# Summing expert rows: fourteen pairs of experts read back early, the last two added by matrix products

## The chip, the core and the metric

The kernel runs on one core of one Trainium2 chip. Time is the device time of an execution in microseconds (us); what counts is the median of several runs. TensorE is called PE, VectorE DVE, ScalarE ACT, GpSimd POOL and SyncE SP, as the profile does.

## The reference, cut to what matters

One transformer block on 512 tokens of width 1024 in f32: modulation from a conditioning vector, an RWKV-7 mixer and a sparse attention mixer, their gated merge, and a mixture of 32 experts, of which each token takes 2.

```python
def hier_moe(u, w_rg, b_rg, w_re, b_re, w_gate, w_up, w_down):
    ...
    top_v, top_i = lax.top_k(in_grp, EXPERT_TOPK)        # 2 of the 8 experts of the best group
    comb = grp_w * jax.nn.softmax(top_v, axis=-1)        # the two weights of a token
    ...
    def expert_block(args):
        xblk, e = args
        hid = jax.nn.silu(xblk @ w_gate[e]) * (xblk @ w_up[e])   # 1024 -> 512
        return hid @ w_down[e]                                   # 512 -> 1024
    ...
    y = jax.ops.segment_sum(yb * buf_w[:, None], buf_tok, num_segments=N + 1)[:N]
...
h = h + gt2 * hier_moe(u2, ...)
return rmsnorm(h, norm_final_g)
```

## The kernel before

The program is a row of blocks (stages) in which each engine has its own list of instructions, ordered by semaphores that are written out by hand. The last stage holds the merge of the mixers, the router, the experts and the final norm; most of the change is in it.

**Tiles of tokens.** The 512 tokens are NT = 4 tiles of 128. `h` keeps the residual, one row of 1024 per token.

**Router.** DVE computes for each token and each of its two choices an entry: a block and a place in that block. Blocks 0 to 15 are pairs of experts (64 places for each of the two), blocks 16 to 30 are spare ones for experts with more than 64 tokens (overflow). From one-hot tables (`at_place`, `oh_blk`) and bf16 products on PE come the tables `slots` (which token lies in place p of block b) and `y_at` (in which of the 1024 rows of `y_dram` its result belongs: choice j, token t). Overflow is counted into `over` (`r_ov`); `further` (L1806) holds a loop over the 15 spare blocks for every engine, skipped by a branch when the count is 0, as it is here. The tables of the router lie in `uT`, which is also the ninth slot of the ring of weights.

**Experts.** For each of 16 pairs `b`: POOL gathers the 128 token rows (`gather`, L1895), PE transposes them (`tokens`, L2354), multiplies by the gate and up weights (`product`, L2368), two experts at a time in the two column halves of the array, ACT applies silu, DVE multiplies (`gated`, L2171), PE transposes the hidden rows (L2378), ACT copies them (L1983), PE multiplies by the down weights (`down`, L2388) in two column halves of 512, DVE multiplies each half by the modulation row into `yo` (`finish`, L2180), and POOL stores the rows of the pair into `y_dram` by an indirect transfer (`store`, L1902).

**Order of weights.** SP issues 96 loads of 2 MB, in order, into a ring of nine slots (`load_expert`, L1786). Each waits until its slot is given back (`unit_free`); the first round waits for other things: the ninth slot for `r_ent` and `r_ov`, since the router's tables lie there. Everything on SP stands in one list, so a load that waits holds back all that follow.

**End.** When all 16 stores have landed, SP passes the overflow branch and reads `y_dram` back in eight loads `ya[2i + j]` of 512 KB (tile i, choice j), into `uT` and `mg`. For each tile DVE adds both with the token's weights into `h` (`summed`, L2216 and L2218), ACT squares and takes a root (L2006, L2008), DVE norms into `ya[2i]` (`normed`, L2224) and SP writes it out (L1876).

The first stage streams the modulation and input weights; POOL loads small parameters there and then waits until about 195 us. `vrep` is a 128x512 buffer of zeros, set by POOL near 37 us and written by DVE much later, in the compressed attention part (L679).

## Time and profile before

| | |
|---|---|
| median of 3 runs | 1309.2 us (1309.09 to 1310.15) |
| profiled execution, time | 1306.26 us |
| profiled execution, span | 1304.4 us |
| mean granted clock of PE | 0.918 |
| PE busy | 1125.7 us (86%) |
| DVE / ACT / POOL busy | 388.4 / 219.2 / 162.6 us |
| mean transfer rate | 231 GB/s |

The span is the time from the first to the last instruction of the profiled execution. Busy time of PE is that of instructions that overlap in a pipeline, so a high share of it doesn't yet say that PE is the limit. An engine's idle time is put down to what it waited for last. A matrix product in f32 shows as two records.

### The profile page before, as it was taken

The numbers are of one execution on the slowest core, as the hardware profiler recorded it, in microseconds if no ns is written. First come the engines' busy times: TensorE is split into PE (matmuls) and PEld (weight loads), VectorE is DVE, ScalarE is ACT, GpSimd is POOL, SyncE is SP. The second block draws the span as 40 slices with busy tenths as digits, with TensorE's granted clock in tenths as the row PEclk, the third lists the DMA queues.
The fourth block names the chain that finished last, engine by engine and source line by source line (L and its number), as shares of the span: only waits on it lengthen the run. The fifth ranks groups of instructions, "written<-read, shape, count | busy, mean of one in ns | idle before, by whom it ended". The sixth has DMA issues, their size and how long they took to land. (4 is left out here: it accounts for less than half of the span.)

```text
span 1304.4 us, 16842 instructions
## 1 busy us (share of the span) xinstructions
PE 1125.7 (86%) x7213; PEld 583.3 (45%) x7213; DVE 388.4 (30%) x644; ACT 219.2 (17%) x443; POOL 162.6 (12%) x211
## 2 busy tenths in 40 slices
PE   6999999999998897989899993988988878887771
PEld 5543344644555555979645451333323333333330
DVE  3244427233005444345522335111111101111105
ACT  4011213221003552424200120000000000000002
POOL 2100001050102443223100000010000000000000
PEclk7899999799996997989899995989989998888995
DMA  9512534325605000000082536999999999999975
GB/s 363 201 65 96 200 114 169 129 85 184 183 26 136 1 1 26 4 2 4 19 311 96 219 124 263 400 428 427 427 427 427 429 426 427 428 427 427 427 297 204
DMA packets 56757, 295.17 MB, mean 226 GB/s; under 512 B 8755, under 2 KB 15253, under 8 KB 43113
## 3 DMA queue, kind: packets, MB, share of 16 engines
q1 hardware_dynamic: 48362, 278.02, 53.3%
q0 software_dynamic: 6016, 11.87, 2.5%
q10 hardware_dynamic: 2304, 4.20, 0.8%
q8 instruction: 58, 0.95, 0.3%
q14 instruction: 17, 0.14, 0.0%
HBM read 284.61 MB, written 16.79 MB: 231 GB/s over the span
## 5 line engine op out<-in xcount | busy, mean ns | idle before, releaser
L2368 PE MATMUL ps<-ring,zrT 128*64 128x512 f32 x704 | 169.4, 638 | 33.3 <-issue 30.4
L894 PE MATMUL ps<-ring,uT 128*128 128x512 f32 x384 | 168.6, 596 | 0.6 <-PE ps L825 0.6
L2388 PE MATMUL ps<-ring,hdT 128*64 128x512 f32 x352 | 122.4, 632 | 6.0 <-issue 4.0
L2368 PEld LDWEIGHTS ps<-ring,zrT 128*64 128x64 f32 x704 | 58.1, 146 | 135.6 <-issue 135.1
L885 PE MATMUL ps<-uT,ring 128*128 128x512 f32 x256 | 115.1, 608 | 2.0 <-DVE uT L619 1.4
L894 PEld LDWEIGHTS ps<-ring,uT 128*128 128x128 f32 x384 | 72.1, 191 | 91.5 <-issue 91.5
L2171 DVE TENSOR_TENSOR zrT<-zrT,ps 128x512 f32<-128x512 f32 x16 | 11.0, 687 | 289.0 <-PE ps L2368 289.0
L2368 PE MATMUL ps<-mg,zrT 128*64 128x512 f32 x160 | 73.2, 612 | 7.4 <-issue 7.4
L885 PEld LDWEIGHTS ps<-uT,ring 128*128 128x128 f32 x256 | 49.0, 194 | 67.4 <-issue 66.4
L1977 ACT ACTIVATE zrT<-ps 128x512 f32<-128x512 f32 x16 | 9.6, 597 | 412.6 <-PE ps L2368 412.6
L1902 POOL DMA_INDIRECT y_dram<-zrT,y_at x16 | 16.3, 1017 | 437.1 <-DVE zrT L2180 437.1
L2388 PEld LDWEIGHTS ps<-ring,hdT 128*64 128x64 f32 x352 | 37.8, 146 | 56.1 <-issue 55.7
L2312 PE MATMUL ps<-ring,uT 128*128 128x512 f32 x128 | 55.8, 593 | 0.0
L969 POOL TENSOR_SCALAR prob<-prob,gate,rsum 128x512 f32<-128x512 f32 (+3 forms) x64 | 40.2, 639 | 117.1 <-DVE rsum L1023 116.2
L2180 DVE TENSOR_TENSOR zrT<-ps,mod 128x512 f32<-128x512 f32 x32 | 22.1, 692 | 106.0 <-PE ps L2388 106.0
L2368 PE MATMUL ps<-mod,zrT 128*64 128x512 f32 x80 | 38.0, 631 | 7.1 <-issue 7.1
L587 DVE SCALAR_TENSOR_TENSOR acc<-ring,csil,acc 128x512 f32<-128x512 f32 x56 | 42.2, 753 | 2.0
L2354 PE MATMUL ps<-cst,zrT 128*128 128x128 f32 x128 | 22.0, 325 | 23.7 <-DMA zrT<-u_dram,slots 23.7
L2388 PE MATMUL ps<-uT,hdT 128*64 128x512 f32 x80 | 37.7, 627 | 4.2 <-issue 4.2
L1046 ACT ACTIVATE prob<-ps,mx 128x512 f32<-128x512 f32 (+3 forms) x64 | 33.2, 523 | 44.8 <-DVE mx L1019 44.5
L2388 PE MATMUL ps<-mod,hdT 128*64 128x512 f32 x80 | 39.2, 647 | 0.0
L1019 DVE TENSOR_REDUCE mx<-ps 128x2 f32<-128x1024 f32 (+3 forms) x32 | 26.4, 824 | 36.9 <-PE ps L1100 36.7
(383 smaller groups left out, 1478.0 us busy)
## 6 DMA issues: line engine op xcount, KB each, us to landing
ring<-in_moe_w_gate_dram SPq DMA_DIRECT2D x22, 2048.0 KB, 30.0
ring<-in_moe_w_up_dram SPq DMA_DIRECT2D x22, 2048.0 KB, 33.6
ring<-in_moe_w_down_dram SPq DMA_DIRECT2D x22, 2048.0 KB, 32.7
ring<-in_w_in_dram SPq DMA_DIRECT2D x8, 2048.0 KB, 13.9
ring<-in_w_ada_dram SPq DMA_DIRECT2D x8, 2048.0 KB, 9.2
mod<-in_moe_w_up_dram SPq DMA_DIRECT2D x5, 2048.0 KB
mg<-in_moe_w_up_dram SPq DMA_DIRECT2D x5, 2048.0 KB, 30.8
uT<-in_moe_w_down_dram SPq DMA_DIRECT2D x5, 2048.0 KB, 36.0
```

Source lines behind the costliest of these rows:

```text
L587: link(dve.scalar_tensor_tensor(a, w[:, k, :], csil[:, k:k + 1], a, ALU.mult, ALU.add))
L885: ins = pe.matmul(ps[:, n % 4, :], slot(name, KD, w)[:, k, c0:c0 + P], uT[:, k, :], start=(k == 0), stop=(k == KD - 1))
L894: ins = pe.matmul(ps[:, n % 4, :], uT[:, k, P * i:P * i + P], w, start=(k == 0), stop=(k == KD - 1))
L969: ins = pool.tensor_scalar(p_, p_, gate[:, i, h3:h3 + 1], rsum[:, t % 4, g:g + 1], ALU.mult, ALU.mult)
L1019: dve.tensor_reduce(mx[:, t % 4, :], ps[:, 2 * (t % 2):2 * (t % 2) + 2, 0:rows_of(t)], AX, ALU.max, negate=True).then_inc(a_mx, 1)
L1046: ins = act.activation(prob[t % 4][:, g, 0:n], ps[:, 2 * (t % 2) + g, 0:n], ACT.Exp, bias=mx[:, t % 4, g:g + 1], accum_out=rsum[:, t % 4, ...
L1902: pool.indirect_dma_start(y_dram, bass.IndirectOffsetOnAxis(ap=y_at[:, b:b + 1], axis=0), yo[:, b % 2, :], None, bounds_check=2 * T - 1, o ...
L2180: dve.tensor_tensor(yo[:, b % 2, 512 * c:512 * c + 512], ps[:, 2 + c, :], mod[:, 5, 512 * c:512 * c + 512], ALU.mult).then_inc(e_y, 1)
L2312: ins = pe.matmul(ps[:, 4 + n % 3, :], mgT[:, k, P * i:P * i + P], slot(f"wo{k // 4}", 4, D)[:, k % 4, 512 * j:512 * j + 512], start=(k == ...
L2354: ins = pe.transpose(ps[:, 4 + k // 4, P * (k % 4):P * (k % 4) + P], src[:, k, :], ident)
L2368: ins = pe.matmul(ps[HALF * r:HALF * r + HALF, "gu".index(kind), :], xgT[:, b % 2, k, HALF * r:HALF * r + HALF], w[r][:, k, :], start=(k = ...
L2388: ins = pe.matmul(ps[HALF * r:HALF * r + HALF, 2 + c, :], hdT[:, j, HALF * r:HALF * r + HALF], w[r][:, j, 512 * c:512 * c + 512], start=(j ...
```

## The change

1. The eight loads of `ya` are issued by SP right after the last weight load, as soon as the stores of pairs 0 to 13 have landed and the slots `uT` and `mg` are given back. Pairs 14 and 15 are no longer stored.
2. `y_dram` is filled with zeros at the start, from `vrep`, by one POOL transfer of 4 MB, since the rows of the last two pairs are read without being stored.
3. The router also makes `w_at` (the weight of each place of each block), by splitting the weights into three bf16 parts and 24 products, and `tok_at`. The load into the ninth slot waits for these products (`r_wt`) in place of `r_ent`.
4. `places` builds for pairs 14 and 15 a matrix place x token that holds the weight where the place has that token; PE multiplies it with `yo` of these pairs. The sums of tile 3 go by PE too, with the two weights on diagonals.
5. DVE does `summed(0)` between the two halves of the last `finish`, `summed(1)` and `summed(2)` behind it, and then `whole(i)`, which adds PE's products from two banks.
6. The last down weights are loaded by column halves, and the last `down` waits for each half apart.
7. The overflow loop (not entered here) adds by the same kind of products.

```diff
+                pool.wait_ge(c_v0, 2)
+                pool.dma_start(y_dram.rearrange("(p b) (a d) -> p (b a) d", p=P, a=2),
+                               vrep[:, :].unsqueeze(1).to_broadcast([P, 4 * T // P, 512])).then_inc(c_fill, 16)
...
                 elif turns == 0 and s_ == 8:
-                    eng.wait_ge(r_ent, 1)
+                    eng.wait_ge(r_wt, 1)
                     eng.wait_ge(r_ov, 1)
...
-                load_expert(sp, "d", NPAIR - 1)
+                for c in range(2):
+                    for half in range(2):
+                        s_, turns = place_of("d", NPAIR - 1, half)
+                        if c == 0:
+                            sp.wait_ge(unit_free[s_], turns + fills[s_])
+                        sp.dma_start(expert_slot(s_, 4)[:, :, 512 * c:512 * c + 512],
+                                     dn[2 * NPAIR - 2 + half][:, :, 512 * c:512 * c + 512])\
+                            .then_inc((unit_in[s_], d_rest[half])[c], 16)
+                for q_ in range(2):
+                    sp.wait_ge(y_st[q_], 16 * (NPAIR // 2 - 1))
+                    s_, turns = place_of("g", NPAIR - 1, q_)
+                    sp.wait_ge(unit_free[s_], turns + 1 + fills[s_])
+                for i in range(NT):
+                    for j in range(2):
+                        sp.dma_start(ya[2 * i + j], y_rows[i, j]).then_inc(f_in[2 * i + j], 16)
...
                     if b + 2 < NPAIR:
                         gather(b + 2)
-                    store(b)
+                    if b < NPAIR - 2:
+                        store(b)
...
+                link(TT(w_blk[:, :, :], oh_blk[:, :, :], wts[:, :, :].rearrange("p j i -> p (j i)").unsqueeze(2)
+                        .to_broadcast([P, 2 * NT, NBLK]), ALU.mult))
+                for m in range(2):
+                    link(dve.tensor_copy(w_part[:, m, :, :], w_blk[:, :, :]))
+                    link(TT(w_blk[:, :, :], w_blk[:, :, :], w_part[:, m, :, :], ALU.subtract))
+                dve.tensor_copy(w_part[:, 2, :, :], w_blk[:, :, :]).then_inc(r_wp, 1)
...
+                def places(b):
+
+                    e_link(dve.scalar_tensor_tensor(toks[:, :], C("tile_down")[:, 0:NT], float(P),
+                                                    tok_at[:, b:b + 1].to_broadcast([P, NT]), ALU.mult, ALU.add))
+                    e_link(TT(matrix(b), C("iota").unsqueeze(1).to_broadcast([P, NT, P]),
+                              toks[:, :].unsqueeze(2).to_broadcast([P, NT, P]), ALU.is_equal))
+                    e_link(TS(matrix(b), matrix(b), w_at[:, b:b + 1], None, ALU.mult))
+                    dve.sem_inc(e_mat, 1)
...
+                finish(NPAIR - 1, 0)
+                summed(0)
+                finish(NPAIR - 1, 1)
+                for i in range(1, NT - 1):
+                    summed(i)
...
+                def whole(i):
+                    dve.wait_ge(f_c, i + 1)
+                    dve.tensor_tensor(h[:, i, :], h[:, i, :], two_banks(i), ALU.add).then_inc(f_h, 1)
...
+                        if b == NPAIR - 1 and c:
+                            for half in range(2):
+                                pe.wait_ge(d_rest[half], 16)
...
                 tokens(0)
+                pe.wait_ge(r_wp, 1)
+                for m in range(3):
+                    for n in range(2 * NT):
+                        ins = pe.matmul(ps[:, 3, 2 * NBLK:3 * NBLK], at_place[:, n, :], w_part[:, m, n, :],
+                                        start=(m + n == 0), stop=(m == 2 and n == 2 * NT - 1))
+                ins.then_inc(r_wt, 1)
...
+                further(pe, first, body, last)
+                pe.wait_ge(e_y, 2 * NPAIR)
+                pe.wait_ge(e_mat, 2)
+                for i in range(NT):
+                    if i == NT - 1:
+                        pe.wait_ge(e_diag, 2)
+                        for j in range(2):
+                            pe.wait_ge(f_in[2 * i + j], 16)
+                    for c in range(2):
+                        cols = slice(512 * c, 512 * c + 512)
+                        terms = [(diag[:, j, :], ya[2 * i + j][:, cols]) for j in range(2)] if i == NT - 1 else []
+                        terms += [(matrix(b)[:, i, :], yo[:, b % 2, cols]) for b in (NPAIR - 2, NPAIR - 1)]
+                        for m, (one, rows) in enumerate(terms):
+                            ins = pe.matmul(ps[:, bank_of[i] + c, :], one, rows, start=(m == 0), stop=(m == len(terms) - 1))
+                    ins.then_inc(f_c, 1)
```

## Rows read from the trace of the kernel before

**Rows 1.** The page, GB/s moved in each of 40 slices of 32.6 us.

```profile
GB/s 363 201 65 96 200 114 169 129 85 184 183 26 136 1 1 26 4 2 4 19 311 96 219 124 263 400 428 427 427 427 427 429 426 427 428 427 427 427 297 204
```

**Rows 2.** Who SP waited for, whole span: us in total, times, longest.

```profile
SPq L1808 <- DMA y_dram<-zrT,y_at: 44.2, 1, 44.2
```

**Rows 3.** Windows: length; PE, PEld, DVE, ACT, POOL busy; PE clock; transfer share, GB/s.

```profile
1252.00:1253.00 1.00, 1.00 (x7) 0.38 (x5) 0.00 (x0) 0.00 (x0) 0.00 (x0) 1.00 1.03 426
...
1261.00:1262.00 1.00, 1.00 (x8) 0.47 (x6) 0.00 (x0) 0.00 (x0) 0.00 (x0) 1.00 0.46 197
...
1286.00:1287.00 1.00, 0.00 (x0) 0.00 (x0) 0.96 (x2) 0.00 (x0) 0.00 (x0) 0.50 1.00 397
```

**Rows 4.** Timeline, last products: start, duration, engine, line, operation, [idle before, releaser].

```profile
1258.42 7.09 PE L2388 MATMUL ps<-ring,hdT 128*64 128x512 f32 x32 [2.68 <-issue]
...
1268.20 7.09 PE L2388 MATMUL ps<-ring,hdT 128*64 128x512 f32 x32 [2.01 <-DMA ring<-in_moe_w_down_dram]
...
1266.23 0.60 ACT L1983 ACTIVATE hdT<-ps 128x512 f32<-128x512 f32 x1 [19.57 <-PE ps L2378]
...
1275.54 0.69 DVE L2180 TENSOR_TENSOR zrT<-ps,mod 128x512 f32<-128x512 f32 x1 [2.95 <-PE ps L2388]
```

**Rows 5.** Timeline of POOL, SP and DVE behind them.

```profile
1237.29 1.02 POOL L1902 DMA_INDIRECT y_dram<-zrT,y_at  x1 [28.25 <-DVE zrT L2180]
...
1281.27 0.33 SPq L1870 DMA_DIRECT2D uT<-y_dram  x1
...
1297.08 1.28 DVE L2218 SCALAR_TENSOR_TENSOR h<-mg,wts,h 128x1024 f32<-128x1024 f32 x1
...
1300.11 1.28 DVE L2224 SCALAR_TENSOR_TENSOR uT<-h,frt,mod 128x1024 f32<-128x1024 f32 x1
```

**Rows 6.** From issue to landing: the 16 stores and 8 row loads; the first row load.

```profile
DMA to landing us min/median/max: 3.2/10.3/11.3
...
uT<-y_dram SPq DMA_DIRECT2D x1, 512.0 KB, 3.6
```

**Rows 7.** Timeline of PE, first stage: products with 128 columns of weights.

```profile
70.54 20.84 PE L885 MATMUL ps<-uT,ring 128*128 128x512 f32 x48 [0.30 <-PE ps L885]
```

**Rows 8.** The overflow branch's first instruction: duration in ns, start.

```profile
L1809 PEldq TENSOR_LOAD <-over x1: 489/489/489, 1270.8 to 1270.8; - x1
...
L1809 DVEq TENSOR_LOAD <-over x1: 547/547/547, 1275.6 to 1275.6; - x1
```

**Rows 9.** Windows of the first stage, columns as in rows 3.

```profile
40.00:42.00 2.00, 2.00 (x3) 0.71 (x3) 2.00 (x6) 0.00 (x0) 0.00 (x0) 0.50 1.02 306
...
48.00:50.00 2.00, 2.00 (x6) 0.85 (x5) 0.00 (x0) 0.32 (x1) 0.00 (x0) 1.00 1.06 389
```

**Rows 10.** Timeline at the router's end: DVE, PE, SP.

```profile
796.08 0.41 DVE L2132 TENSOR_TENSOR uT<-cst,uT 128x248 f32<-128x248 f32 x1
...
801.30 0.42 DVE L2159 CAST over<-uT 1x16 int32<-1x16 f32 x1
...
797.66 0.40 PE L2345 MATMUL ps<-uT 128*128 128x31 bf16 x8
803.78 1.97 PE L2354 MATMUL ps<-cst,zrT 128*128 128x128 f32 x8 [5.72 <-DMA zrT<-u_dram,slots]
807.16 15.40 PE L2368 MATMUL ps<-ring,zrT 128*64 128x512 f32 x64 [1.41 <-DVE zrT L2163]
...
801.82 0.33 SPq L1786 DMA_DIRECT2D uT<-in_moe_w_down_dram  x1
815.78 0.33 SPq L1786 DMA_DIRECT2D ring<-in_moe_w_down_dram  x1
```

**Rows 11.** Windows there, columns as in rows 3.

```profile
780.00:785.00 5.00, 1.63 (x8) 1.49 (x7) 2.96 (x13) 0.21 (x1) 0.00 (x0) 0.50 0.98 414
...
808.00:810.00 2.00, 2.00 (x8) 0.79 (x6) 0.00 (x0) 0.00 (x0) 0.00 (x0) 0.50 0.75 297
...
812.00:814.00 2.00, 2.00 (x12) 0.78 (x10) 0.00 (x0) 0.00 (x0) 0.00 (x0) 1.00 0.01 4
```

More of the change, by code:

```diff
@@ L1753, in build @@
         order = (1, 2, 0, 5, 3, 4, 6, 7, 8)
-        x_clear, r_ya, r_ent = sem("x_clear"), sem("r_ya"), sem("r_ent")
+        x_clear, r_ya, r_ent, r_wp, r_wt = (sem(n) for n in ("x_clear", "r_ya", "r_ent", "r_wp", "r_wt"))
+        e_mat, e_diag, e_wat, e_dve, f_c = (sem(n) for n in ("e_mat", "e_diag", "e_wat", "e_dve", "f_c"))
+        d_rest = [sem(f"d_rest{n}") for n in range(2)]
+        v_tok, v_wt, v_m1, v_m2, v_m, v_cm, v_c = (sem(f"v_{n}") for n in "tok wt m1 m2 m cm c".split())
         y_rows = y_dram.rearrange("(j i p) d -> i j p d", j=2, p=P)
@@ L1860, in body @@
                     sp.sem_inc(v_seen, 1)
-                def last():
-                    sp.wait_ge(v_st, 16 * OVER)
-                for q_ in range(2):
-                    sp.wait_ge(y_st[q_], 16 * (NPAIR // 2))
-                further(sp, first, body, last)
-                for i in range(NT):
-                    for j in range(2):
-                        sp.dma_start(ya[2 * i + j], y_rows[i, j]).then_inc(f_in[2 * i + j], 16)
+                further(sp, first, body)
                 sp.wait_ge(m_wr, 80)
@@ L2141, in _ @@
                 dve.tensor_tensor(slots[:, :], hi[:, :], ps[:, 2, 0:NBLK], ALU.add).then_inc(r_sl, 1)
+                link(dve.scalar_tensor_tensor(tok_at[:, :], hi[:, :], -float(T), ps[:, 2, 0:NBLK], ALU.add, ALU.add))
                 dve.wait_ge(r_ent, 1)
@@ L2171, in gated, with finish @@
                     dve.tensor_tensor(hd, act_g, ps[:, 1, :], ALU.mult).then_inc(e_hd, 1)
-                def finish(b):
-                    for c in range(2):
+                def finish(b, *one):
+                    for c in one or range(2):
                         dve.wait_ge(e_d, 2 * b + c + 1)
@@ L2190, in _, with summed @@
                     finish(b - 1)
-                finish(NPAIR - 1)
+                    if b == NPAIR - 2:
+                        dve.wait_ge(e_wat, 1)
+                        places(NPAIR - 2)
+                        places(NPAIR - 1)
+                        for j in range(2):
+                            dve.tensor_scalar(diag[:, j, :], C("ident"), wts[:, j, NT - 1:NT], None, ALU.mult)\
+                                .then_inc(e_diag, 1)
+                f_link = Chain(dve, f_dve)
+                def summed(i):
+                    for j in range(2):
+                        dve.wait_ge(f_in[2 * i + j], 16)
+                        f_link(dve.scalar_tensor_tensor(h[:, i, :], ya[2 * i + j], wts[:, j, i:i + 1], h[:, i, :], ALU.mult,
+                                                        ALU.add))
+                finish(NPAIR - 1, 0)
[3 more added lines that the diff above has]
+                    summed(i)
                 def first():
-                    for q_ in range(2):
-                        dve.wait_ge(y_st[q_], 16 * (NPAIR // 2))
+                    pass
                 def body(v):
@@ L2224, in normed @@
                     dve.scalar_tensor_tensor(ya[2 * i], h[:, i, :], frt[:, i:i + 1], gf, ALU.mult, ALU.mult)\
                         .then_inc(f_o, 1)
-                summed(0)
+                whole(0)
                 for i in range(1, NT):
-                    summed(i)
+                    whole(i)
                     normed(i - 1)
```

83 lines of the change are left out of this document (57 added, 26 removed).

## The prediction

> **What bounds the kernel now.** I read the transfer line of the page first. From 820 us on it stands near 427 GB/s in every slice [rows 1]: the sixteen pairs of experts are bound by the stream of their weights, and PE, though busy on the page, waits for it. What comes before sets when that stream starts, what comes after is added to its end. So I read two places: the head of the last stage, and everything behind the last weights. The matrix "who waited for whom" of SP's queue gives the second: after its last weight load SP sits 44.2 us in the wait for the stored rows [rows 2].
>
> The windows of the tail show that the last weights don't end at once: 426 GB/s at 1252 and 197 at 1261 [rows 3]. Some of the 16 transfer engines are done long before the slowest, and have nothing to do, since the rows are only asked for at 1281. The timeline then gives the chain [rows 4, 5]: the down product of the last pair starts at 1268.20, released by its weights, and ends near 1275.3; DVE scales its second half at 1275.54; POOL stores it; SP reads all rows back from 1281.27; DVE adds two rows to each of four tiles (1.28 us each), the last add starts at 1297.08 and ends at 1298.37; the last normed tile ends at 1301.39, and the span ends at 1304.4, 3.05 later.
>
> **The change at the end, part by part.** *Last down weights by halves.* The 4.19 MB of the last pair's down weights are the last in the queue. At 427 GB/s they take 9.8 us, so they arrive from 1258.4 to 1268.2. In runs of 2 KB the only rows I have are those of the first stage, 389 GB/s at 48 to 50 [rows 9]: 10.8 us, end 1269.2. The other bound is the 306 GB/s at 40 to 42, where small transfers were mixed in: 13.7 us, end 1272.1. I take the first, since nothing small is queued at the end. The first column half is there by 1265.3 even by the slow bound, before the transposed hidden rows, which ACT delivers at 1266.83 [rows 4]. So the first half of the product starts at 1266.9 instead of 1268.2, the second follows 3.55 us later, at 1270.45, if its weights are there (they are, by 1.3 us; by the slow bound they are 1.7 late, which would cost 1.7). DVE began its second half 7.34 us after the product's start [rows 4]: 1266.9 + 7.34 = 1274.2, against 1275.54. **Gain 1.3.**
>
> *Rows of fourteen pairs fetched early.* The store of pair 13 is issued at 1237.29, and stores land within 11.3 us [rows 5, 6]: SP can issue the eight row loads from 1248.6 at the latest, some 4 us in all. They stand in the queue behind the weights, so the fast engines take them in the tail that now is empty, and the slowest at 1269.2. A load of 0.52 MB at 397 GB/s [rows 3] takes 1.3 us: the first two land at 1270.5 and 1271.8, the eighth at 1279.7.
>
> *A wait is added on DVE.* It runs: first half of the last pair (2.95 + 0.69 before the second [rows 4], so 1270.6 to 1271.3), then the sums of tile 0, which wait for these two loads, then the second half of the last pair. The two sums take 2 x 1.31 = 2.6: 1273.9, and the second half is due at 1274.2. No loss, with 0.3 to spare in DVE's time and 0.8 in the landing of the second load (1271.8 against 1272.6). Behind that wait stand the second half and so PE's final products. The second half ends at 1274.9. Tiles 1 and 2 are summed to 1280.1; the branch on the overflow count then costs DVE 1.0 (its load of 0.55 and three register steps, which before lay beside the last scaling [rows 8]): DVE is free at 1281.2.
>
> *Final place-token products.* They take the place of two stores, and PE had nothing to do there. A 128x512 product with 128 columns of weights in f32 shows as two records; 48 records took 20.84 us [rows 7], 0.433 each. Tiles 0 to 2 have 4 products, tile 3 has 8, since both sums of tile 3 go by products too: 20 products, 40 records, 17.5 us with the last one's end. PE starts when both halves are scaled, at 1274.95; its own branch runs ahead of the matmuls in flight. Tiles are ready at 1278.6, 1282.0, 1285.5 and **1292.5**. DVE adds tile 0 from 1281.2 and the next two with their norms by 1289.6, so the fourth waits for PE: the path is PE's. An add of 128x1024 from the products' bank is priced between 1.28 (the SBUF form [rows 5]) and 2 x 0.69 [rows 4], I take 1.28: 1293.8. From the last sum's end to the end of the last normed tile were 3.02 us (1298.37 to 1301.39), and 3.05 to the span's end; nothing of that changes: 1293.8 + 3.02 + 3.05 = **1299.9**, against 1304.4. **Sum: -4.5 us.** So the early fetch removes the store, its landing and the read, about 10 us, and PE's products give back more than half of it.
>
> **The change elsewhere.** *Fill of the row buffer (4.2 MB written by POOL after its set-up loads, in the second slice).* A slice of 32.6 us can carry 13.9 MB at 427 GB/s; the second and third carry 6.6 and 2.1 [rows 1]. So it fits, and PE's input products, which run on from 70.54 with no wait for a transfer [rows 7], keep their cover. Its end is waited for at the reuse of its source only in the attention part. Cost 0.
>
> *Weights by entry in the router.* DVE gets one op before the count (0.2) and six of 0.41 (248 elements a partition [rows 10]) after the count's last op at 801.30: ready at 804.4. PE gets 24 bf16 products of 31 columns behind the first transposes, which end at 805.75; 8 such took 0.40, so 1.0 to 1.2: done at 806.9. PE then waited for DVE's copy until 807.16 anyway [rows 10]. Cost 0; bounds 0 and +0.5 if a weight load isn't hidden. The eighth slot's load, though, waits for them: it moves from 801.82 to 807.0. The next load is only issued at 815.78, when the first gate product gives its slot back, and from 810 the transfers stand still (4 GB/s at 812 to 814 [rows 11]): 2.1 MB need 5 us and are there by 814. Cost 0, and the price if that cover were gone is up to 5.2 us, since all later weights queue behind.
> *Masks, diagonals* on DVE before the last gated product: some 3 us between the scaling of pair 13 and the gating of pair 15, with two products of PE as long as the 7.09 us of [rows 4] in between. Cost 0.
>
> The profiled execution took 1306.26 us for a span of 1304.4; the median of the runs is 1309.2, 2.9 above it. I apply the difference to the median: 1309.2 - 4.5 = **1304.7**.
>
> **The Trainium skill.** At the head, the granted clock is 0.50 until 810 and full after it [rows 11], while PE was busy from 803.78 to 805.75 and again from 807.16 [rows 10]; the 24 new products fill the hole. The Trainium skill, "TensorE: Matmul & The Clock Gate", Part 1, says that the clock is throttled by default and that activity releases it; by that rule the hole filled may bring the full clock before the gate product, which is the rival early clock below. [...]
> For the tail, the same notes (the Trainium skill, "DMA: Bandwidth & Descriptors", Latency and other measured facts) say that two of the sixteen engines are usually slower; the falling rate of [rows 3] agrees that some are, and the sum above already takes the slowest.
>
> **Rivals.** *Early clock:* 2.9 us of the first gate product at full instead of half speed (807.16 to 810.1) bring the release at 815.78, and with it the whole stream, 1.5 forward: 1303.2. For: the hole is filled. [...] 0.2.
> *Rows late:* the sums of tile 0 hold the last scaling back. If the first row load lands 3.6 us after the last weights, as the first one did on empty queues [rows 6], the second lands at 1274.1, the last half is scaled 1.2 later: 1305.9; at worst some 2 more. For: the slowest engine decides. Against: queued loads landed at the pace of the stream. 0.15.
> *A clock drop in the final products:* PE pauses 0.7 us before and 1.0 us after the last down product; before, pauses of 2.0 and 2.7 [rows 4] left the clock full. One short stretch at half speed costs 1.7 to 2.5: 1306.4 to 1307.2. 0.1.
> *Slower, by the clock:* if the clock stays low, the products take twice 17.5 us. It decides from a low stretch of 9 us on (half of it is lost, against 4.5 gained); all of it gives 1322. For it: PE's clock drops once it is idle. Against it: no long pause is left. 0.07.
> *The slot's load delays the stream:* decides if the entry products end after 811 (their rows late, POOL's gather late). Up to 1309.9. 0.05.
> *The change doesn't do what it says:* the early row loads aren't early, because SP gets to them late, or the product of tile 3 isn't the last thing DVE waits for. Then PE's 17.5 us stand behind the loads: about 1308. 0.03.
> The forecast has the remaining 0.4.
>
> **The numbers.** Likeliest 1304.7. The range takes the early clock and 0.7 of scatter below (1302.5), and above the late rows and a clock drop together with the router's 0.5: 1304.7 + 1.2 + 2.5 + 0.5 = 1308.9 (the slow bound of the halves, 1.7, lies within). A measurement of this kernel tells some 0.2% from no change, 2.6 us: faster means below 1306.6. Forecast and early clock are there, most of the late rows, and a part of the drop: 0.72. Within 0.2%: 0.19. Slower: the low clock and the larger part of the unknown: 0.09.
>
> **What would show it.** (1) The last scaling on DVE near 1274.2, behind two sums of tile 0 with at most a few tenths of waiting for rows. (2) The final products: 40 records in about 17.5 us at full clock, starting within 0.2 us of the last scaling, and DVE's fourth add released by PE. (3) No loads of weights later at the head: the issue now at 815.78 unmoved (or 1.5 earlier: early clock). (4) The transfer rate high up to 1270 and beyond instead of falling from 1254. Wrong would be: PE waiting for tile 3's rows, the clock at 0.5 in the products, or the first gate product starting later than 807.2.

## The result

| kernel | median | lowest to highest | ratio, 95% interval |
|---|---|---|---|
| before, beside it | 1309.68 us (4 runs) | 1309.09 to 1310.17 | |
| after | 1302.05 us (4 runs) | 1301.26 to 1303.23 | 0.9943 [0.9925, 0.996] |

The change makes the kernel 7.6 us faster. The forecast was 1304.7 us, 4.5 faster, with a range down to 1302.5: the direction was right, the gain was larger than the whole range allows. The profiled execution of after took 1302.55 us for a span of 1300.7, at a mean granted clock of 0.935.

### The profile page after: what moved, and what is told of

The parts are those of the page before. It is cut to its first block and busy times, and to the rows that moved or that the text cites. A ratio compares the mean times of both kernels' runs of the same rounds, so it can differ in the third digit from the quotient of the medians.

```text
span 1300.7 us, 16995 instructions
## 1 busy us (share of the span) xinstructions
PE 1137.6 (87%) x7277; PEld 589.9 (45%) x7277; DVE 396.5 (30%) x662; ACT 218.7 (17%) x443; POOL 161.8 (12%) x210
## 5 line engine op out<-in xcount | busy, mean ns | idle before, releaser
L2448 PE MATMUL ps<-ring,zrT 128*64 128x512 f32 x704 | 163.2, 618 | 28.5 <-issue 26.3
```

Of the source, the lines that this page charges most:

```text
L2448: ins = pe.matmul(ps[HALF * r:HALF * r + HALF, "gu".index(kind), :], xgT[:, b % 2, k, HALF * r:HALF * r + HALF], w[r][:, k, :], start=(k = ...
```

## The profile after

The transfer line of the page, one number for 32.5 us, answers [rows 1].

```profile
GB/s 365 330 65 97 197 108 180 129 74 189 190 24 139 1 1 26 4 3 4 5 326 57 250 92 279 363 429 431 428 430 429 428 430 428 429 431 429 430 391 147
```

Two things are seen at once. The second slice carries 330 instead of 201 GB/s, which is the fill. And the slices of the weight stream, which the change doesn't touch, stand at 428 to 431, where before they stood at 426 to 429. I had read this line only for "the stream is the bound"; half of the surprise is in its last digit.

The head, timelines of SP and of PE [rows 10]:

```profile
807.69 0.33 SPq L1799 DMA_DIRECT2D uT<-in_moe_w_down_dram  x1
818.29 0.33 SPq L1799 DMA_DIRECT2D ring<-in_moe_w_down_dram  x1
```

```profile
806.81 0.85 PE L2479 MATMUL ps<-uT 128*128 128x31 bf16 x24
808.43 6.79 PE L2448 MATMUL ps<-ring,zrT 128*64 128x512 f32 x18 [0.76 <-DVE zrT L2199]
```

The 24 new products take 0.85 us inside the hole before the gate product; the ninth slot's load goes out at 807.69 (807.0 was forecast). The clock in the gate product (windows, columns as in rows 3):

```profile
812.00:814.00 2.00, 2.00 (x8) 0.66 (x6) 0.00 (x0) 0.00 (x0) 0.00 (x0) 0.52 0.99 424
814.00:816.00 2.00, 2.00 (x12) 0.72 (x10) 0.00 (x0) 0.00 (x0) 0.00 (x0) 1.00 0.55 221
```

It stays at half speed until nearly 814. In the profile of before it was full in 812 to 814 already [rows 11]; a second profile of the same kernel (before_again, below) has it as late as after has, with 0.60 in that stretch, and starts its gate product and the next load of weights as late:

```profile
808.62 3.68 PE L2368 MATMUL ps<-ring,zrT 128*64 128x512 f32 x8 [1.41 <-DVE zrT L2163]
818.24 0.33 SPq L1786 DMA_DIRECT2D ring<-in_moe_w_down_dram  x1
```

The last products and the final ones, PE's timeline [rows 4]:

```profile
1249.52 8.78 PE L2448 MATMUL ps<-ring,zrT 128*64 128x512 f32 x32 [2.64 <-issue]
1259.27 7.09 PE L2471 MATMUL ps<-ring,hdT 128*64 128x512 f32 x32 [0.96 <-issue]
1266.28 0.75 PE L2458 MATMUL ps<-cst,zrT 128*128 128x128 f32 x4
1267.95 7.09 PE L2471 MATMUL ps<-ring,hdT 128*64 128x512 f32 x32 [0.92 <-ACT hdT L2011]
```

DVE's timeline over the same stretch and to the end [rows 4, 5]:

```profile
1271.64 0.69 DVE L2216 TENSOR_TENSOR zrT<-ps,mod 128x512 f32<-128x512 f32 x1 [4.35 <-PE ps L2471]
1272.25 1.28 DVE L2253 SCALAR_TENSOR_TENSOR h<-uT,wts,h 128x1024 f32<-128x1024 f32 x1
1273.56 1.29 DVE L2253 SCALAR_TENSOR_TENSOR h<-mg,wts,h 128x1024 f32<-128x1024 f32 x1
1275.27 0.69 DVE L2216 TENSOR_TENSOR zrT<-ps,mod 128x512 f32<-128x512 f32 x1 [0.42 <-PE ps L2471]
...
1282.73 2.35 DVE L2299 TENSOR_TENSOR h<-h,ps 128x1024 f32<-128x1024 f32 x2 [1.61 <-issue]
...
1293.49 1.22 DVE L2299 TENSOR_TENSOR h<-h,ps 128x1024 f32<-128x1024 f32 x1 [2.64 <-PE ps L2547]
...
1296.45 1.28 DVE L2304 SCALAR_TENSOR_TENSOR uT<-h,frt,mod 128x1024 f32<-128x1024 f32 x1
```

And the chain that ended last, same stretch (start, length, what):

```profile
1275.27 0.70 DVE zrT L2216
1275.97 0.04 issue
1276.02 17.45 PE ps L2547 x40
1293.47 0.02 issue
1293.49 1.23 DVE h L2299
```

The final products stand in it as one piece of 17.45 us. SP's queue, behind the last gate and up loads:

```profile
1226.91 31.55 SPq L1879 DMA_DIRECT2D ring<-in_moe_w_down_dram  x4
1258.64 2.27 SPq L1888 DMA_DIRECT2D uT<-y_dram  x1
...
1265.36 0.60 SPq L1888 DMA_DIRECT2D mg<-y_dram  x1
```

The row loads go out from 1258.64, not from 1248.6, since the last down weights, by halves, hold the queue. The line of 31.55 us joins four issues; behind the first lies a wait for a free slot, and the third alone takes 18.24 us (the four by themselves, shortest, median and longest in ns):

```profile
L1879 SPq DMA_DIRECT2D ring<-in_moe_w_down_dram x4: 557/1773/18237, 1226.9 to 1255.6; - x4
```

The rows land 10.9 to 14.0 us after their issue, the first two loads at 1270.8 and 1271.9 us and the eighth at 1279.4, where 1270.5, 1271.8 and 1279.7 were forecast. The transfer rate of the tail against [rows 3]:

```profile
1261.00:1262.00 1.00, 1.00 (x8) 0.48 (x6) 0.00 (x0) 0.00 (x0) 0.00 (x0) 1.00 1.05 406
...
1272.00:1273.00 1.00, 1.00 (x7) 0.35 (x5) 1.00 (x2) 0.00 (x0) 0.00 (x0) 1.00 1.02 418
1273.00:1274.00 1.00, 1.00 (x7) 0.36 (x5) 0.96 (x2) 0.00 (x0) 0.00 (x0) 1.00 0.77 307
```

406 GB/s at 1261 where 197 were: the tail is filled with rows, as said.

## The experiments

All times are medians, with the ratio to the kernel before on the same chip in the same batch. Where batches are compared I go by ratios.

| kernel | median | ratio, 95% |
|---|---|---|
| before_again | 1309.25 | 0.9996 [0.9983, 1.001] |
| before_head | 1309.31 | 0.9995 [0.998, 1.0009] |
| before_halves | 1310.34 | 0.9996 [0.9982, 1.0011] |
| after_whole_down | 1302.73 | 0.9946 [0.9926, 0.9966] |
| before_pad64 | 1305.96 | 0.9976 [0.9968, 0.9985] |
| after_pad64 | 1305.77 | 0.9969 [0.9957, 0.9981] |
| after_dve_tile3 | 1302.21 | 0.9935 [0.9923, 0.9947] |
| after_late_rows | 1308.15 | 0.9992 [0.9984, 1.0001] |
| before_pad32 | 1309.91 | 1.0003 [0.9991, 1.0014] |
| before_pad64_halves | 1306.13 | 0.9973 [0.9962, 0.9984] |
| after_split_tile3 | 1299.77 | 0.9926 [0.9913, 0.9939] |
| before_pad192 | 1308.76 | 0.9988 [0.9979, 0.9996] |
| before_slots_only | 1306.49 | 0.9977 [0.9967, 0.9987] |
| before_rest_only | 1309.51 | 1.0002 [0.9991, 1.0013] |
| before_ring0 | 1305.23 | 0.9965 [0.9952, 0.9978] |
| before_ring64 | 1306.42 | 0.9978 [0.997, 0.9987] |

### The parts alone

**before_again** is the kernel before, unchanged, for a second profile of it.

> The kernel before, unchanged, timed against itself: it shows how its profiled executions differ and what its time is made of. Theory 1 (the missing 3 us lie in the execution that I read: 1306.26 us where the runs have 1309.1 to 1310.2, so some term that my sum took from its trace is longer in the usual execution): ratio 1.000 within 0.001, and a profiled execution that is longer than 1306.3 shows the extra time in one place, either the head (issue of the tenth weight load later than 815.78 us) or the end of the weight stream (last down product later than 1268.20). Theory 2 (the new kernel's parts are each worth more than I said): its profile looks as the first one.

Measured 1309.25 us, the profiled execution 1309.32. Its last products on PE:

```profile
1261.02 8.62 PE L2388 MATMUL ps<-ring,hdT 128*64 128x512 f32 x32 [2.68 <-issue]
1271.21 7.09 PE L2388 MATMUL ps<-ring,hdT 128*64 128x512 f32 x32 [0.89 <-ACT hdT L1983]
```

The profile that I had read was of a quick execution (1306.26 us), and it differs where it mattered. There the fifteenth down product took 7.09 us and the last one waited 2.01 us for its weights [rows 4]; here the fifteenth takes 8.62, in part at half clock (0.83 in the mean of 1260 to 1270 us), and the last waits 0.89 us for ACT's hidden rows, its weights being there. Two chains end within 1.5 us of each other, and which is last changes with where the clock drops for a moment. Of the 3 us by which the first execution was quicker, 2.5 lie ahead of the stream (its first issue at 815.78 against 818.24).

**before_head**: the fill and the router's weights by entry, with the two tiles that these need.

```diff
+                pool.dma_start(y_dram.rearrange("(p b) (a d) -> p (b a) d", p=P, a=2), ...).then_inc(c_fill, 16)
...
+        tok_at, w_at = (alloc(top, n, [P, NBLK]) for n in ("tok_at", "w_at"))
...
-                    eng.wait_ge(r_ent, 1)
+                    eng.wait_ge(r_wt, 1)
...
+                for m in range(3):
+                    for n in range(2 * NT):
+                        ins = pe.matmul(ps[:, 3, 2 * NBLK:3 * NBLK], at_place[:, n, :], w_part[:, m, n, :], ...)
```

> The kernel before with the fill of the row buffer and the weights by entry in the router (products behind the first transposes, the ninth slot's load waiting for them), the end left as it was. My prediction: no change, 0 us (at most +0.5). Rival, early clock: 1.5 to 3 us faster than the kernel before, with the granted clock at 1.0 sooner after the first gate product. If the ninth slot's load delays the stream: up to 5 us slower.

Ratio 0.9995: no cost; the interval reaches from 2.6 us quicker to 1.2 slower. The next load of weights went out at 818.73 us, in before_again at 818.24. Fill, entries and the later ninth load are hidden, as costed.

**before_halves**: only the last down weights by halves.

```diff
-                load_expert(sp, "d", NPAIR - 1)
+                for c in range(2):
+                    for half in range(2):
+                        ... sp.dma_start(expert_slot(s_, 4)[:, :, 512 * c:512 * c + 512], ...)
...
+                        if b == NPAIR - 1 and c:
+                            for half in range(2):
+                                pe.wait_ge(d_rest[half], 16)
```

> The kernel before with the last down weights loaded by column halves, all else as before. My prediction: 1.3 us faster, the last down product starting with ACT's hidden rows and not with the weights. Rival: nothing, if transfers in runs of 2 KB make the last half so late that its product ends where it did; then the last scaling stays where it was after the pair's hidden rows.

Ratio 0.9996, no gain. The interval alone would still leave room for the forecast 1.3 us; it is the profile that speaks against them: its last down product waits 0.89 us for ACT, as in before_again. **after_whole_down** is the converse, after without this edit.

> The new kernel with the last down weights loaded whole again, all else as in it. By my steps it loses the 1.3 us of the halves: near 1303.4 us, 0.9952 of the kernel before. If the halves are worth nothing once PE's own chain is the later one at the end (down product of pair 14 ending after the weights are there): no change against the new kernel's 1302.05.

0.9946 against after's 0.9943. Its queue, then the four joined issues by themselves:

```profile
1217.15 18.98 SPq L1799 DMA_DIRECT2D ring<-in_moe_w_down_dram  x4
1248.85 0.33 SPq L1881 DMA_DIRECT2D uT<-y_dram  x1
```

```profile
L1799 SPq DMA_DIRECT2D ring<-in_moe_w_down_dram x4: 327/380/432, 1217.1 to 1235.8; - x4
```

No issue takes more than 0.43 us here; the rest of the 18.98 us is waiting for free slots. With whole loads the rows are asked for at 1248.85, as forecast, ten us earlier than in after, and it is worth nothing: in both they are there when DVE comes.

### The place of the weight slots

None of this explains 7.6 us. Counted from the issue behind the ninth slot's load (815.78 in [rows 10], 818.24 in before_again, 818.29 in after), the last down product and the last scaling on DVE start after

| | last down product | last scaling |
|---|---|---|
| before, before_again | 452.4, 453.0 us | 459.8, 460.3 us |
| after | 449.7 us | 457.0 us |
| before_pad64 | 450.6 us | 457.9 us |
| after_pad64 | 453.0 us | 460.3 us |

So 3.3 us of the gain are there before the last scaling, where the forecast had 1.3. The change allocates small tiles ahead of `uT2`, `ring2` and `mg`, which hold five of the nine slots. Tiles are placed in steps of 32 bytes, so that `tok_at` and `w_at` take 128 bytes each of every partition, and `ovw` (weights of the overflow) and `toks` (for `places`) 32 each. The first two make 256 together; the 64 of the other two are what moves the slots, from 192 bytes behind a multiple of 256 to a multiple of 256 within each partition. (before_head has `tok_at` and `w_at` alone, and its weights stream at 427 GB/s, as in before.) Two kernels move the slots alone:

```diff
+        pad = alloc(top, "pad", [P, 16])
         uT = alloc(top, "uT2", [P, KD, T])
```

> The kernel before with one unused tile of 64 bytes a partition allocated ahead of uT2; nothing else. It moves the weight slots (ring2) and all behind them by 64 bytes, to addresses divisible by 128, where the changed kernel's own small tiles put them. Place theory: the weight stream of the kernel before is slowed because its slots begin 64 bytes off a multiple of 128. Then this kernel streams as the changed one does: against the start of the ninth slot's issue, the last pair's gate product starts near 431.2 us instead of 433.0 us, the pause of PE before the fifteenth down product shrinks from 2.7 us to about 1 us, that product takes 7.1 us and not 8.6 us, the last scaling comes 2.5 to 3.5 us sooner, and the median is 1306 to 1307 us. Rival, traffic theory: the stream is quicker in the changed kernel because of other work (the rows, the head, the halves), and this kernel measures 1309.3 us with the gate product at 433.0 us.

> The changed kernel with the same unused 64 bytes a partition ahead of uT2, so that its slots are again 64 bytes off a multiple of 128, as in the kernel before. Place theory: it loses what the kernel before gains by its padding: the last pair's gate product at 433.0 us after the ninth slot's issue instead of 431.2 us, a median of 1304.5 to 1305.5 us, which is what the forecast's own terms gave (1304.7 us). Traffic theory: no difference, 1302.0 us.

Both came out as the place theory says: 1305.96 and 1305.77. Padding takes 0.24% off the kernel before and gives 0.26% back to the kernel after, 3.1 and 3.4 us. The windows 860 to 1220 us of before, before_pad64, after_pad64 and after, in this order (last column GB/s):

```profile
860.00:1220.00 360.00, 297.24 (x1286) 112.33 (x1284) 39.44 (x48) 13.03 (x24) 24.33 (x24) 0.92 1.01 427
```

```profile
860.00:1220.00 360.00, 294.42 (x1294) 114.59 (x1292) 39.45 (x48) 13.03 (x24) 24.31 (x24) 0.94 1.01 429
```

```profile
860.00:1220.00 360.00, 299.77 (x1292) 114.29 (x1288) 39.45 (x48) 12.23 (x23) 24.34 (x24) 0.92 1.01 427
```

```profile
860.00:1220.00 360.00, 292.67 (x1293) 112.46 (x1290) 39.43 (x48) 13.03 (x24) 24.32 (x24) 0.94 1.01 429
```

427, 429, 427, 429: it goes with the place, not with the change. In the trace's records of single transfers of 16 KB between 840 and 1225 us, 38% take 611 ns in before and the others mostly 612 to 620 (mean 614.9); in before_pad64 and after 96 to 97% take 611 (mean 612.2). That is 0.44%, 1.8 us of the 405 us in which the stream runs. More comes with it. The last gate and up product of before_slots_only and the down product behind it, and those of before_again above, show how:

```profile
1250.54 8.78 PE L2370 MATMUL ps<-ring,zrT 128*64 128x512 f32 x32 [2.64 <-issue]
1260.22 7.09 PE L2390 MATMUL ps<-ring,hdT 128*64 128x512 f32 x32 [0.90 <-issue]
```

In seven of the eight profiles with the slow stream (the exception is that of before) the fifteenth down product is the one that runs partly at half clock (8.5 to 8.8 us), behind a pause of 2.7 us, and the last one then waits for ACT (0.89 us), not for weights. In the ten with the quick stream the fifteenth takes 7.09 each time; the drop, where there is one, falls into the product ahead of it, and there it is covered by the wait for weights. Stream and drop together make the 2.4 us by which before_pad64 starts its last down product sooner than before_again. The other 0.7 to 1.0 of 3.1 to 3.4 I have not followed to a line; the intervals leave room for it.

Which property of the place it is, six more kernels ask. **before_pad32** has `[P, 8]` in place of `[P, 16]`, **before_pad192** `[P, 48]`:

> The kernel before with an unused tile of 32 bytes a partition ahead of uT2: the weight slots then begin 96 bytes behind a multiple of 128. If only a multiple of 128 counts, this one streams no quicker than the kernel before (last pair's gated product 440.3 us or later behind the ninth slot's issue; 1309.3 us). If each odd 32 or 64 bytes costs something of its own, it lies above 1309.3 us, by up to the 3.5 us that 64 bytes cost. If the gain of the 64-byte padding came from anything else than where the slots lie on a multiple of 128 (that all small tiles behind it moved), it could come here too: 1306 us.

> The kernel before with 192 bytes of padding: the weight slots behind it then begin at a multiple of 128 bytes that is no multiple of 256 (with 64 bytes of padding they begin at multiples of 256). If a multiple of 128 is what counts, this kernel equals the one with 64 bytes: 1306.0 us, 429 GB/s in 860 to 1220 us. If it takes a multiple of 256, it equals the kernel before or is slower: 1309.3 us or more, 427 GB/s. The Trainium skill, DMA: Bandwidth & Descriptors, How a descriptor splits into AXI transactions, says that a transfer that doesn't begin at a multiple of 256 bytes costs the beats from the boundary below it; by that rule the second would come, and more so than with 64 bytes. A row of this case speaks against it: the slots of the first ring begin 128 bytes off a multiple of 256 in every kernel, and in the changed kernel the whole stream runs at 429 GB/s with them.

Pad32 gains nothing (1.0003, 427 GB/s). Pad192, which puts the slots 128 bytes behind a multiple of 256, gains about half in time (0.9988, 0.9979 to 0.9996), between the two theories, though its stream is the slow one:

```profile
860.00:1220.00 360.00, 301.20 (x1292) 114.18 (x1288) 39.46 (x48) 12.21 (x23) 24.31 (x24) 0.91 1.01 427
```

So a multiple of 128 isn't enough. For these slots the page's side of the expectation came nearer: the Trainium skill, "DMA: Bandwidth & Descriptors", How a descriptor splits into AXI transactions, says that a transfer's pieces start at multiples of 256 bytes and that one which begins elsewhere costs the beats from the boundary below. These runs agree as far as the place of `uT2`, `ring2` and `mg` goes. The row that I set against it stands all the same, as the first ring shows below.

**before_slots_only** and **before_rest_only** part the slots from the tiles behind them (`hdT` first):

```diff
+        pad = alloc(top, "pad", [P, 16])         # slots_only, with [P, 48] ahead of hdT; rest_only has only [P, 16] there
         uT = alloc(top, "uT2", [P, KD, T])
...
+        pad_h = alloc(top, "pad_h", [P, 48])
         hdT_ = alloc(top, "hdT", [P, EH])
```

> The kernel before with 64 bytes of padding ahead of uT2 and 192 bytes more ahead of hdT: the slots in uT2, ring2 and mg begin at multiples of 256 bytes, the tiles behind them (hdT, the router's weights, statistics) lie as before within 256 bytes. Theory that the slots' own place as the destination of the weights counts: as with 64 bytes of padding, 1306.0 us and 429 GB/s in 860 to 1220 us. Rival, that the place of hdT counts (PE reads it as weights in each down product): as before, 1309.4 us and 427 GB/s.

> The converse: 64 bytes of padding only ahead of hdT; the slots lie as before, 192 bytes behind a multiple of 256, and hdT at a multiple of 256. Theory of the slots: 1309.4 us, 427 GB/s. Rival of hdT: 1306.0 us, 429 GB/s.

0.9977 at 429 GB/s against 1.0002 at 427: it is the slots. Whether they count as what the transfers write or as what PE reads, no run parts. **before_ring0** and **before_ring64** shift the first ring by 128 or 64 bytes and keep the rest as in before_pad64:

```diff
+        pad_a = sb("pad_a", [P, 32])             # ring64: 16 here, 48 behind
         ring = sb("ring", [P, RP, SLOT])
+        pad_b = sb("pad_b", [P, 32])
```

> The kernel before with 64 bytes ahead of uT2 and with the first ring moved by 128 bytes (128 more behind it), so that all nine slots begin at multiples of 256. If a slot at 128 bytes behind a multiple of 256 costs what the four others cost with 192 bytes of padding, the three slots of the first ring cost some 2 us in the kernel with 64 bytes of padding, and this one measures about 1304 us with more than 429 GB/s. If the first ring is quick where it lies, 1306.0 us and 429 GB/s.

> As the last, but the first ring moved by 64 bytes: its three slots begin 192 bytes behind a multiple of 256, as ring2, uT2 and mg do in the kernel before, and these lie at multiples of 256. If each slot at such a place costs the same, three of nine cost three fifths of the 3.3 us that five cost: about 1308.0 us, 428 GB/s. If what counts is only ring2, uT2 and mg, 1306.0 us and 429 GB/s.

The three slots of the first ring don't behave like the others. At 192 bytes behind a multiple of 256 they should cost some 2 us and cost none (0.9978, 429 GB/s; 94% of the 16 KB transfers at 611 ns, in before_pad64 97%); at a multiple of 256 they gain perhaps 1.4 us (0.9965 against 0.9976, the intervals overlap; 99% at 611 ns). Why moving `ring2`, `uT2` and `mg` is worth so much and moving `ring` so little stays open.

The records of single transfers show that it isn't only a matter of where each one lands. Between the last landing of one load and the first of the next, all sixteen transfer engines carry the same load, so that its 16 KB transfers can be told by slot; such stretches lie between 840 and 1097 us. The share of them that took 611 ns, in the order in which the slots are filled (`mg` has too few such records; the slow kernels are before, before_again, before_head, before_halves, before_rest_only and after_pad64, the quick ones all but before_ring0 and before_ring64, which move `ring`):

| slots | place | six at 427 GB/s | eight at 429 GB/s |
|---|---|---|---|
| `mod` | multiple of 256 in all | 98% | 100% |
| `uT2` | 192 behind, or a multiple of 256 | 34% | 99% |
| `ring`, three slots | 128 behind in all | 44, 52, 12% | 98, 96, 90% |
| `ring2`, three slots | 192 behind, or a multiple of 256 | 2, 67, 2% | 96, 99, 99% |

Transfers into `ring` lie in the same place in all of these kernels, and yet they slow down with the others; those into `mod` hardly do. So the place of the five slots decides how the stream runs, but a cost that each transfer pays for its own start doesn't describe it, and the mechanism isn't shown.

**before_pad64_halves** joins the two edits, to ask for the halves again where the profile has the last product waiting for weights.

> The kernel before with the 64 bytes of padding and the last down weights by halves, as in the changed kernel. In the profile of the padded kernel the last down product waits 1.99 us for its weights and starts 1.1 us later than the hidden values allow (0.89 us behind PE's transposes wherever these set it). Theory that halves pay exactly where the weights come last: the wait falls to 0.9 us and the median to about 1304.9 us, 1.1 us under the padded kernel's 1306.0 us. Rival, that they are worth nothing in any place because the second halves still land where the wholes did, or because four short-run loads take the queue longer: 1306.0 us.

The line of before_pad64, then that of before_pad64_halves:

```profile
1267.82 7.09 PE L2389 MATMUL ps<-ring,hdT 128*64 128x512 f32 x32 [1.99 <-DMA ring<-in_moe_w_down_dram]
```

```profile
1268.92 7.09 PE L2400 MATMUL ps<-ring,hdT 128*64 128x512 f32 x32 [0.89 <-ACT hdT L1992]
```

The wait does fall from 1.99 to 0.89 us, and the last scaling comes 457.1 us behind the start of the stream instead of 457.9. after against after_whole_down is the same picture: released by ACT at 0.92 us, 457.0, against weights waited for 2.02 us, 457.9. So the profiles give the halves 0.8 to 0.9 us, but only with the quick stream; the ratios give 0.4 in both places (0.9973 and 0.9976, 0.9943 and 0.9946), which their intervals don't part from nothing. The halves and the place of the slots go together: in seven of the eight profiles with the slow stream the last product waits for ACT whatever its weights do.

### The tail

**after_late_rows** has one more wait ahead of the row loads:

```diff
+                sp.wait_ge(e_d, 2 * NPAIR - 1)
```

> The changed kernel with one wait added: SP issues the loads of the expert rows (fourteen pairs) only when the last down product's first half is done, and no longer behind the fourteenth pair's stores. It shows what the early place of these loads is worth and what the wait for a second row load on DVE, ahead of the second scaling, costs. By the landing times of 11 to 14 us the loads, issued from about 1272 us, land from 1275 to 1286 us and later; the scaling of the second half waits for the second of them (about 1276.5 us) and the sums and outputs follow the rows as in the kernel before: 4 to 8 us later than the changed kernel, 1306 to 1310 us. If the early issue is worth only the queue's own time (1.5 us for each load), it measures 1304.3 us; if the rows bound nothing, 1302.0 us.

1308.15 us, 6.1 above after and in the range given. DVE:

```profile
1274.81 1.28 DVE L2254 SCALAR_TENSOR_TENSOR h<-uT,wts,h 128x1024 f32<-128x1024 f32 x1 [4.01 <-DMA uT<-y_dram]
```

The final products, and the clock in them (windows):

```profile
1278.42 13.15 PE L2548 MATMUL ps<-zrT 128*128 128x512 f32 x24 [4.93 <-DVE zrT L2217]
```

```profile
1279.00:1284.00 5.00, 5.00 (x7) 1.88 (x6) 4.41 (x4) 0.00 (x0) 0.00 (x0) 0.54 0.63 254
```

DVE waits 4.0 us for the rows, and the last scaling falls 3.5 us back (460.5 behind the start of the stream, 457.0 in after). PE, idle for 4.93 us ahead of the final products, runs them at 0.54 of its clock at first: 24 records take 13.15 us, 2.6 more than the 10.57 of after. 3.5 + 2.6 is the 6.1 measured. From the last scaling to the end of the span this profile has 28.0 us where after has 25.4. Both rivals of the tail, rows late and clock drop, are thus real mechanisms, and late rows bring the drop with them.

**after_dve_tile3** moves both row sums of the fourth tile back to DVE, **after_split_tile3** one of them:

```diff
-                for i in range(1, NT - 1):
+                for i in range(1, NT):            # dve_tile3; split_tile3 adds only ya[6] here
                     summed(i)
...
-                        terms = [(diag[:, j, :], ya[2 * i + j][:, cols]) for j in range(2)] if i == NT - 1 else []
+                        terms = [(diag[:, 1, :], ya[2 * i + 1][:, cols])] if i == NT - 1 else []   # dve_tile3: none
```

> The changed kernel with the last two pairs' rows of the fourth token tile summed on DVE, as for the second and third, and without the 16 products by diagonal matrices. Theory that PE's final products set the end (40 records, 17.45 us, the last scaled sum starting 1.2 us behind them): 24 records take 10.4 us, PE is done near 1286.5 us and the last place products no longer bound; DVE then has two more sums of 1.3 us and ends its chain itself: sums until 1283.7 us, then 2.35 + 2.35 + 1.28 us for the last two outputs of the lower tiles, and the fourth tile's two, so that it gains 0 to 1.5 us: 1300.6 to 1302.0 us, most likely 1301.3 us. Rival: DVE's chain is the longer one already, or its waits grow; the two added sums of 1.3 us then come on top and it measures 1303.5 to 1304.7 us.

1302.21 us, no gain and no loss, between the two that I had given. With both on PE, DVE waits 2.64 us for the fourth tile and ends 22.46 us behind the start of the last scaling (1275.27 to 1297.73). With both on DVE, the chain that ended last is DVE's, with ACT's squares between (start, length, what):

```profile
1282.70 1.30 DVE h L2253
1284.03 0.55 DVEq L1834
...
1296.58 1.29 DVE uT L2304
```

It ends 22.37 us behind the last scaling at 1275.50. The forecast's chain on PE and the other one on DVE are equal to 0.1 us, which asks for a split.

> The changed kernel with one of the fourth token tile's two row sums on DVE and the other still on PE by a diagonal matrix. With both on PE, PE ends last and DVE waits 2.6 us for it; with both on DVE, DVE ran without a gap to the end and the time was the same (1302.2 us). Theory that the two chains then ended within 0.1 us of each other: DVE has 1.3 us less than in the second, PE 8 records less than in the first, so that the end comes 1.0 to 1.3 us earlier than in either: 1300.9 us (1300.7 to 1301.2). Rival: something else sets the end in both (the output's store, the branch ahead of the last outputs), and it stays at 1302.1 us.

Its last lines on PE and on DVE:

```profile
1290.64 1.88 PE L2549 MATMUL ps<-zrT 128*128 128x512 f32 x4
```

```profile
1276.06 0.69 DVE L2216 TENSOR_TENSOR zrT<-ps,mod 128x512 f32<-128x512 f32 x1 [0.43 <-PE ps L2474]
...
1292.86 1.21 DVE L2302 TENSOR_TENSOR h<-h,ps 128x1024 f32<-128x1024 f32 x1
...
1295.82 1.28 DVE L2307 SCALAR_TENSOR_TENSOR uT<-h,frt,mod 128x1024 f32<-128x1024 f32 x1
```

The end is 21.04 us behind the last scaling, 1.4 less than in after, near what the theory of the two chains says (1.0 to 1.3). The median, 1299.77, is 2.3 less than after's, but the ratios don't part the three kernels: 0.9926 (0.9913 to 0.9939) against 0.9943 (0.9925 to 0.9960) and 0.9935 (0.9923 to 0.9947). So the shorter chain is seen in one profile, and a gain in time is likely and not shown.

## Why the forecast was off

**The sum of what was forecast against what it made.** At the old place of the slots the change measures 0.9969 (after_pad64), 4.1 us of gain against 4.5 forecast: 1305.4 by the ratio for 1304.7. The miss is a term that the prediction doesn't have, 3.4 us for the place of the slots. The step that failed is "*The change elsewhere*", where the new small tiles (`tok_at` and `w_at`, and `ovw` and `toks`, whose 64 bytes do the moving) appear only with their instructions, if at all. The place of the slots was put at nothing without being looked at; before_pad64 and after_pad64 measure it at 3.1 and 3.4 us. An allocation is an edit too: it moved five of the nine destinations of the 96 weight loads. Why the place matters stays open.

That 4.1 lies so near to 4.5 is in part luck. In after_pad64 the last down product starts 453.0 us behind the issue, as in before_again, so that the halves gave nothing of their 1.3, and the tail gave more than its 3.2.

**Halves, −1.3: wrong.** The term was read from one wait of 2.01 us [rows 4] in an execution that was 3 us quicker than the median. In before_again the same product waits for ACT, and the edit alone measured 0.9996. Only together with the quick stream do the profiles show a worth, 0.8 to 0.9 us; the ratios give 0.4 and can't tell it from nothing.

**Early rows: right in the result, wrong in one step.** "SP can issue the eight row loads from 1248.6" doesn't hold with the halves: the queue was held until 1258.5. The landing was costed by the stream's pace and not by the issue, so the error cost nothing: the first two loads landed within 0.3 us of the forecast, and neither the sums of tile 0 nor the last scaling waited for them.

**The added wait on DVE, no loss: right.** The last scaling is released by PE 0.42 us behind the sums. after_late_rows shows what the wait costs when it isn't covered: 6.1 us.

**Final products: right.** 40 records, 17.45 us (17.5 forecast), from 0.75 us behind the last scaling's start; the fourth add released by PE; 4.24 us from there to the end of the last normed tile (1.28 + 3.02 forecast). From the last scaling to the span's end there were 28.9 us before and 25.4 after: the tail gives 3.4, where the forecast had 3.2. Over the twelve profiles with the old tail that stretch is 28.9 to 29.6, in the mean 29.2, and over the three with the tail of after (after, after_whole_down, after_pad64) 25.5: 3.8 of the 4.1. The branch cost 1.6 us, not 1.0, on DVE, where it wasn't last.

**Head, fill, masks, 0: right** (before_head). By the prediction's own signs it would have been wrong: the issue moved from 815.78 to 818.29, and the gate product started at 808.43, later than 807.2. But before_again, with nothing changed, has 818.24 and 808.62: the signs were set by one quick execution. **Early clock: didn't come;** the clock rose near 814. **Clock drop in the final products: not in after,** where it is 1.00 from 1276 on; it came when PE was idle for 4.93 us. That pauses of 2.0 and 2.7 us leave the clock full held in the one profile that I had read: in before_again the product behind a 2.68 us pause took 8.62 us.

By the profiles, before_again against after, both near their medians (1309.32 and 1302.55 us): 6.8 us, of which 3.3 lie before the last scaling (2.4 the place of the slots, 0.9 the halves that it makes useful) and 3.4 behind it. The medians differ by 0.8 more; 0.4 of that is the old tail's usual length (29.2 us against 28.9 in this profile), the rest no line shows.

## What to carry to other kernels

When a kernel is bound by a stream of transfers, list every tile whose address an edit moves and look at where it then begins: here a move of the destinations by 64 bytes was worth 3.4 us, nearly as much as all the restructuring (4.1). A term that rests on one wait needs a second profile of the same kernel, above all where two chains end within a microsecond or two. And where two engines share the last work, move it until both end together: both extremes measured the same, and the split between them shortened the chain by 1.4 us in its profile.

## What the runs showed of the hardware

- **Place of the slots.** The stream of 2 MB loads (16 KB a partition) runs at 429 GB/s where `uT2`, `ring2` and `mg` begin at a multiple of 256 bytes in the partition, at 427 where they begin 128, 192 or 224 behind one. Moving `ring` by 64 bytes, to 192 behind, cost nothing (0.9978 against 0.9976). Transfers into `ring`, unmoved, are slowed together with the others (12 to 52% at 611 ns against 90 to 98%).
- **An issue held by short runs.** The third of four issues of 1 MB in runs of 2 KB took 18.24 us in after; issues of whole loads of 2 MB took 0.33 to 0.43 us at the same point.
- **The clock near a pause.** Of the 22 products of 32 records, in all 18 profiles, that start after 1245 us behind a pause of 2.6 to 2.8 us, twelve took 8.5 to 8.8 us and ten 7.09 (before_pad64: 2.60, then 7.09; after_dve_tile3: 2.63, then 7.09). Behind 4.93 us of idleness (after_late_rows) the clock was 0.54 in the 5 us from 1279.
